# Gated DeltaNet core: masked decay matrices made and stored in the projection

## What is computed

```python
decay = where(tril, exp(g[:, None] - g[None, :]), 0)
L  = where(strict, (k * beta) @ k.T * decay, 0)     # solve (I + L) [u, w] = [v*beta, k*beta*exp(g)]
qk = where(tril, q @ k.T * decay, 0)
q_dec = q * exp(g)
v_new = u - w @ S
o  = q_dec @ S + qk @ v_new
S  = S * exp(g_last) + k_dec.T @ v_new
```

## Time and profile before

| | |
|---|---|
| median of 3 runs | 4827.85 us (4827.19 to 4833.41) |
| the profiled execution, its own time | 4825.45 us |
| its span | 4823.7 us |
| busy, share of the span | PE 86%, PEld 71%, DVE 57%, ACT 43%, POOL 37% |
| mean granted TensorE clock | 0.954 |
| HBM read, written | 369.87 MB, 169.54 MB |
| GDN projection | about 247 to 1562 us |
| delta core | about 1585 to 3310 us |

### The profile page before, as it was taken

How to read it: one execution, slowest core, us unless ns; L and a number is a source line. 1 busy time by engine, 2 the same in 40 slices (tenths; PEclk the granted TensorE clock), 3 DMA queues, 4 the chain that set the end, 5 groups by cost and what they waited for, 6 DMA issues and landing times. The chain is left out here.

```text
span 4823.7 us, 83518 instructions
## 1 busy us (share of the span) xinstructions
PE 4166.8 (86%) x30756; PEld 3447.5 (71%) x30756; DVE 2754.4 (57%) x3377; ACT 2085.9 (43%) x3927; POOL 1768.6 (37%) x1236
## 2 busy tenths in 40 slices
PE   7699999999999688888888888884999779978769
PEld 2278888888887577777777777774888668866657
DVE  3245454554545677777777777775455433228853
ACT  3222222223232566666666666664111421128832
POOL 2222121221211567666777677664111232200022
PEclk8799999999999799999999999997999789998889
DMA  6212221222222444444444444434444324253244
GB/s 224 87 44 76 78 74 57 68 79 74 64 67 68 117 112 112 113 112 114 115 114 111 114 113 111 111 108 159 169 175 176 116 75 142 97 217 137 113 138 136
DMA packets 598327, 541.17 MB, mean 112 GB/s; under 512 B 118688, under 2 KB 562336, under 8 KB 581024
## 3 DMA queue, kind: packets, MB, share of 16 engines
q1 hardware_dynamic: 598208, 539.59, 36.3%
HBM read 369.87 MB, written 169.54 MB: 112 GB/s over the span
## 5 line engine op out<-in xcount | busy, mean ns | idle before, releaser
L555 PE MATMUL pj_bank<-h_hi,pj_whi 128*128 128x512 f32 (+1 forms) x1920 | 717.1, 373 | 19.9 <-POOL pj_wlo L541 18.8
L555 PE MATMUL pj_bank<-h_lo,pj_whi 128*128 128x512 f32 (+1 forms) x1920 | 708.3, 369 | 0.0
L555 PE MATMUL pj_bank<-h_hi,pj_wlo 128*128 128x512 f32 (+1 forms) x1920 | 707.5, 368 | 0.0
L745 ACT ACTIVATE pj_raw<-pj_bank 128x512 f32<-128x512 f32 (+1 forms) x240 | 127.9, 553 | 952.5 <-PE pj_bank L555 473.5
L538 POOL TENSOR_TENSOR pj_whi<-pj_w,ones 128x1024 fp32r<-128x1024 f32 x48 | 115.3, 2402 | 1021.4 <-PE pj_bank L555 1007.1
L555 PEld LDWEIGHTS pj_bank<-h_hi,pj_whi 128*128 128x128 f32 x1920 | 363.3, 189 | 84.3 <-POOL pj_wlo L541 19.3
L1368 DVE TENSOR_TENSOR dc_Y<-dc_psY,dc_pick 128x256 f16<-128x256 f32 x864 | 323.1, 415 | 168.0 <-PE dc_psY L1119 168.0
L1274 ACT ACTIVATE dc_R<-dc_psR 128x256 f16<-128x256 f32 x720 | 245.3, 382 | 396.7 <-PE dc_psR L1135 395.6
L555 PEld LDWEIGHTS pj_bank<-h_lo,pj_whi 128*128 128x128 f32 x1920 | 363.4, 189 | 62.3 <-issue 3.8
L555 PEld LDWEIGHTS pj_bank<-h_hi,pj_wlo 128*128 128x128 f32 x1920 | 363.0, 189 | 60.7
L838 DVE TENSOR_SCALAR pj_acc<-pj_raw,pj_conv_w 128x2307 f32<-128x2307 f32 x32 | 90.8, 2836 | 471.1 <-ACT pj_raw L745 471.1
(11 more groups left out here) (270 smaller groups left out, 10396.6 us busy)
## 6 DMA issues: line engine op xcount, KB each, us to landing
dc_tm<-scratch_tm SPq DMA_DIRECT2D x288, 192.0 KB, 2.5
dc_cgr<-scratch_cgrow SPq DMA_DIRECT2D x288, 128.0 KB, 2.8
dc_fm<-scratch_fm SPq DMA_DIRECT2D x288, 128.0 KB, 2.3
scratch_o<-dc_ob SPq DMA_DIRECT2D x288, 128.0 KB, 2.0
scratch_tm<-pj_tm SPq DMA_DIRECT2D x24, 1152.0 KB, 5.0
pj_w<-in_gdn_w_in SPq DMA_DIRECT2D x48, 512.0 KB, 6.2
scratch_fm<-pj_row SPq DMA_DIRECT2D x16, 1152.0 KB, 5.2
dc_kr<-scratch_fm SPq DMA_DIRECT2D x288, 64.0 KB, 2.6
```

What stands on the lines that cost most here:

```text
L555: i = pe.matmul(self.bank[blk][:, 0:n], l[b][:, k, :], r[:, k, at:at + n], start=(m == 0), stop=(m == 3 * KT - 1))
L745: act.activation(raw_row(raw, blk), pr.bank[blk][:, 0:BLKS[blk][1]], ACT.Silu if KINDS[j] == "z" else ACT.Copy).then_inc(pr.s_ev, 1)
```

## The change

- **Gates:** ScalarE also makes Exp of the rows `cgT` (five groups), which SyncE stores as `egrow` in two pieces before the last store of the phase.
- **Projection:** every tile also makes the decays of three chunks (8 heads x 18 chunks = 144 items in all): SyncE loads the broadcast rows and the gates of the chunk; ScalarE makes Abs of the difference (four of 128 columns, the gate as bias) and Exp; VectorE multiplies by beta and the strict mask (four of 128 columns) into `BD` and by the inclusive mask into `E`; SyncE stores both to DRAM (`decays`). On ScalarE decays 0 and 1 stand ahead of a tile's first `take`, decay 2 ahead of its last; on VectorE all three stand ahead of the tile's convolution or normalisation.
- **`Projection`** (both projections): the raw weights share memory with the low part, so the load waits for TensorE's products of the tile two back; the high part is a plain copy.
- **Core:** differences, Abs, Exp, beta and mask multiplies are gone. SyncE loads `dd` (both decay matrices) and `egr` (the exponentiated row). VectorE makes L and QK straight from the Gram bank, one behind the other, at levels 1 and 2; TensorE reuses the bank after QK. QK has four buffers. ScalarE's high parts move from levels 4 and 5 to 2 and 3; GpSimd keeps `Sd`, `qd`, `vb` and `Llo`. A and the first X stay on VectorE as they were.

```diff
@@ Projection
-        if not first:
-            sp.wait_ge(self.s_split, t - 1)
+        if not first:
+            sp.wait_ge(self.s_mm, t * NB - NB)
...
-        pool.tensor_tensor(self.whi[b][:], self.w32[b][:], self.ones[:].unsqueeze(1).broadcast_to([P, KT, P]),
-                           ALU.mult).then_inc(self.s_whi, 1)
+        pool.tensor_copy(self.whi[b][:], self.w32[b][:]).then_inc(self.s_whi, 1)
@@ phase_project_gdn, SyncE
+                def decays(h, j, last):
+                    store_decay(h, j, 0)
+                    store_decay(h, j, 1)
+                    load_decay(h, j, 2)
...
+                    if not done:
+                        load_decay(*then, 0)
+                    store_decay(h, j, 2)
+                    if not done:
+                        load_decay(*then, 1)
@@ phase_project_gdn, ScalarE
+                def decay(h, j, o):
+                    c, b, k, u = item(h, j, o)
+                    act.wait_ge(d_load[b], u * 48 + 48)
+                    for dr in range(2):
+                        for v in range(2):
+                            i = act.activation(E[b][:, dr, v], E[b][:, dr, v], ACT.Abs, scale=-1.0, bias=gi[b][:, dr, Q_CG, v:v + 1])
+                    i.then_inc(s["d_abs"], 1)
+                    act.wait_ge(s["d_abs"], k + 1)
+                    act.activation(E[b][:], E[b][:], ACT.Exp, scale=-1.0).then_inc(s["d_exp"], 1)
...
                 def stage(h, j, first):
+                    decay(h, j, 0)
+                    decay(h, j, 1)
                     take(h, j, 0, first)
...
+                    decay(h, j, 2)
                     take(h, j, 4, first)
@@ phase_project_gdn, VectorE
+                def decay(h, j, o):
+                    c, b, k, u = item(h, j, o)
+                    dve.wait_ge(s["d_exp"], k + 1)
+                    for dr in range(2):
+                        for v in range(2):
+                            i = dve.scalar_tensor_tensor(BD[b][:, dr, v], E[b][:, dr, v], gi[b][:, dr, Q_BETA, v:v + 1], strict[:, dr],
+                                                         ALU.mult, ALU.mult)
+                    i.then_inc(s["d_scaled"], 1)
+                    dve.wait_ge(s["d_scaled"], k + 1)
+                    dve.tensor_tensor(E[b][:], E[b][:], incl[:].unsqueeze(2).broadcast_to(C4), ALU.mult).then_inc(s["d_done"], 1)
...
                 def stage(h, j, first):
+                    for o in range(PT):
+                        decay(h, j, o)
@@ phase_delta_core, GpSimd
+                    if rec:
+                        for p in range(2):
+                            faded_state(i, q, p)
+                    if inv:
+                        for p in range(2):
+                            faded_q(i + 1, 1 - q, p)
                     for p in range(2):
+                        if inv:
+                            beta_v(i + 1, 1 - q, p)
                         if make:
                             low(i + 2, q, p)
@@ phase_delta_core, TensorE
                     else:
-                        pe.wait_ge(s_gm[0], j + 1)
+                        pe.wait_ge(s_qk[0], j + 1)
...
                     if p == 0:
-                        wait(pe, s_gm[1], i + 3, NI)
+                        wait(pe, s_qk[1], i + 3, NI)
@@ phase_delta_core, VectorE
-                def masked(j, q, p):
...
-                    dve.tensor_tensor(gm[q][p][:], bV[:], sides[:], ALU.mult).then_inc(s_gm[p], 1)
-
-                def scores(j, q, p):
-                    dve.wait_ge(s_bd[p], j + 1)
+                def scores(j, q, r, p):
+                    dve.wait_ge(p_gram[p], j + 1)
+                    dve.wait_ge(ld_d[q][p], of_load(j, q, 2))
                     wait(dve, s_llo[p], j)
-                    dve.wait_ge(s_gm[p], j + 1)
-                    dve.tensor_tensor(L32[p][:], heads(gm[q][p][:, :, 0, :]), bd[p][:], ALU.mult).then_inc(s_L[p], 1)
+                    dve.tensor_tensor(L32[p][:], heads(bV[:, :, 0, :]), dd[q][p][:, :, 1], ALU.mult).then_inc(s_L[p], 1)
+                    wait(dve, p_out[p], j - 3)
+                    dve.tensor_tensor(qk[r][p][:], heads(bV[:, :, 1, :]), dd[q][p][:, :, 0], ALU.mult).then_inc(s_qk[p], 1)
...
                         if make and l in (1, 2):
-                            masked(i + 2, q, l - 1)
+                            scores(i + 2, q, (r + 2) % 4, l - 1)
                         if rec and l == 2:
                             right_side(i, q, 1)
-                        if make and l in (3, 4):
-                            scores(i + 2, q, l - 3)
```

More of the change, by code:

```diff
@@ L353, in _ @@
                 sp.dma_start(dram["cgrow"], cgT[:]).then_inc(s["stored"], 16)
+                sp.wait_ge(s["grown"], len(GROUPS))
+                for at in range(0, TOK, HALF):
+                    n = min(HALF, TOK - at)
+                    sp.dma_start(dram["egrow"][:, at:at + n], grown(at, n)).then_inc(s["stored"], 16)
                 sp.wait_ge(s["pack"], 1)
@@ L442, in _ @@
                 i.then_inc(s["el"], 1)
+                act.wait_ge(s["rows"], KT)
+                for n, at, w in GROUPS:
+                    act.wait_ge(s["row"], n + 1)
+                    act.activation(grown(at, w), cgT[:, at:at + w], ACT.Exp).then_inc(s["grown"], 1)
             @block.vector
@@ L592, in phase_project_gdn @@
         epsq = sb("epsq", [P, 1])
+        C4 = [P, 2, 2, P]
+        E, BD = ([sb(f"{x}{i}", C4) for i in range(2)] for x in ("E", "BD"))
+        gi = [sb(f"gi{i}", [P, 2, NQTY, 2]) for i in range(2)]
+        incl, strict = sb("incl", [P, 2, P], F16), sb("strict", [P, 2, P], F16)
+        dram["decays"] = nc.dram_tensor("scratch_decays", (NQ, NCH, 2, P, 2, 2, P), F32, kind="Internal").ap()
+        d_load, d_out = ([sem(f"pj_d_{x}{i}") for i in range(2)] for x in ("load", "out"))
         aux = [ctx.enter_context(nc.psum_tensor(f"pj_aux{i}", [P, 512], F32)) for i in range(3)]
         names = ("const", "conv0", "conv1", "conv2", "conv", "pads", "silu", "square", "aux", "aux_read", "recip", "norm",
-                 "fm_out", "tm_out", "z_out", "fm_turn")
+                 "fm_out", "tm_out", "z_out", "fm_turn", "sides", "mask", "d_abs", "d_exp", "d_scaled", "d_done")
         s = {q: sem("pj_" + q) for q in names}
@@ L662, in stage @@
                         store_tm(h, "trK", 0)
+                    decays(h, j, last)
                 for j in range(NT):
@@ L674, in _ @@
                 sp.wait_ge(s["z_out"], 32 * nth(NQ - 1, NT - 1, "z"))
+                for b in range(2):
+                    sp.wait_ge(d_out[b], 32 * (NQ * NCH // 2))
             @block.gpsimd
@@ L884, in phase_delta_core @@
         Rf = two("Rf", C4)
-        qk, qd = four("qk", C4), four("qd", C4)
+        qk, qd = [[sb(f"qk{r}{p}", C4) for p in range(2)] for r in range(4)], four("qd", C4)
         vb, xr, vs, vn, ob, Sd = (two(x, C4) for x in ("vb", "xr", "vs", "vn", "ob", "Sd"))
@@ L1000, in step @@
                 def step(m, n, last):
-                    for load, ahead in ((load_rec, 1), (load_fm, 3), (load_row, 4)):
+                    for load, ahead in ((load_rec, 1), (load_fm, 3), (load_decays, 4)):
                         if not (last and n + ahead >= NCH):
@@ L1210, in run @@
                 @sweep
-                def run(i, q, ahead, make, inv, rec):
-                    j, r = i + 1, 1 - q
+                def run(i, q, r, make, inv, rec):
+                    j = i + 1
                     for l in range(1, NLEV):
@@ L1296, in run @@
                 @sweep
-                def run(i, q, ahead, make, inv, rec):
+                def run(i, q, r, make, inv, rec):
                     j = i + 1
-                    if make:
-                        decays(i + 2, q, 0)
                     for l in range(1, NLEV):
@@ L1309, in run @@
                             new_v(i, l - 3)
-                        if make:
-                            if l == 1:
-                                decays(i + 2, q, 1)
-                            elif l <= 3:
-                                growth(i + 2, q, l - 2)
-                            elif l <= 5:
-                                high(i + 2, l - 4)
+                        if make and l in (2, 3):
+                            high(i + 2, l - 2)
                     if rec:
```

164 lines of the change are left out of this document (78 added, 86 removed).

## The result

The changed kernel takes **5023.48 us** (median of 4 runs, 5018.29 to 5025.51) against 4830.44 for the kernel before in the same comparison (4827.19 to 4833.41): a ratio of **1.0398**, 95% interval 1.038 to 1.0416. The forecast was 4891, its range 4802 to 4955. The sign was right; the size was three times what I had.

The account below looks back on a forecast made before the run. The projection was taken as bound by TensorE's products, the delta core by hand-overs with no engine full. Core 25, opening -3, projection 40 and gates 1 gave +63 us on the median 4827.85: 4891 us, range 4802 to 4955.

Parts of the forecast that it names:

- Core, the walk: Delta core step: hand-over delay of 1.2 us less 0.84 us from a shorter X, so 0.36 us a step longer.
- The term of the X: Core, VectorE: first X no longer beside GpSimd's subtraction, 0.42 us instead of 1.26, state 0.84 us earlier.
- The dearer hand-over: Core: two VectorE multiplies instead of one after each Gram product before bank reuse, 1.2 us later at level 3.
- rival 2: Core: freed VectorE swallows the second multiply and the whole 0.88 us wait goes; total 4804 us, chance 0.18.
- rival 3: Core: VectorE not freed of GpSimd, X stays 1.26 us; core +84, total 4950 us, chance 0.14.
- over some 70 steps: Delta core: the 0.36 us of one step multiplied over the core's steps, +25 us.
- I take 5 us a head, eight heads: +40 us: Projection: third decay delays the convolution of K by 4 to 6 us, stalling TensorE; bounds 0 and 72.
- the walk's own terms: Projection, one head: normalisation ends 979.1, decays 0 and 1 by 982.9, decay 2's load lands 988 to 990 us.
- behind it stand silu and square: Projection, after K's late convolution: both end at 1005.82, TensorE's norms begin at 1005.9, so no slack.
- a tile that I had called free: Projection: in tiles Q and V decay 2 was to end about 0.7 us before the convolution.
- None before the norms of Q: Projection: no TensorE idle time expected before the norms of Q, against about 5 us a head before K's.
- The table loads: Projection, ScalarE: 1.28 us each by the row used; at the skill's 2.66, eight heads cost an estimated 11 us more.

Follow-up runs that it names:

- experiment 7: Changed kernel with three row-load buffers, one Gram-bank copy at the hand-over (GpSimd makes QK, loop of two) and second L cast at level 3: 4744.76 us.
- experiment 1: Kernel before with four steps instead of two in the delta core's loop body on every engine: 4870.55 us (1.0083).
- experiment 8: Kernel before, core loop body lengthened: four steps on TensorE only 4872.22 us; four on the other engines only 4831.01; eight on all 4846.31.
- experiment 9: Changed kernel with TensorE's core program written out for all 72 steps, other engines keeping the loop of four: 4963.88 us (1.0277).
- Experiment 4: Changed kernel with three buffers for the projection's loaded rows and two half-size beta buffers: 4884.36 us (1.0112).

## Why the prediction was wrong, and where it was right

**Core, the walk: right.** "1.2 - 0.84 = 0.36 us a step". The term of the X is shown by itself: 0.84 from the one cast. The dearer hand-over has no run of its own; against the kernel of experiment 7 it is 1.20 (23.75 against 22.55), with the other differences named there. The net of the two was 0.19 a step (23.75 against 23.56), 14 us instead of 25. The kernel before is 1.01 above that of experiment 7 and not 0.84, so 0.17 us a step are left that no run assigns. Rivals 2 and 3 are refused by the rows: the second multiply was not swallowed, and VectorE was freed.

**Core, the loop: missed.** The prediction priced "over some 70 steps" by one step and never looked at what the body of four does to TensorE's own program. It costs 50 us of the 62.5, and experiments 1, 8 and 9 show it from both sides. The profile of before could have warned: the 71 step lengths of its core (1625 to 3299 us) hold 17738 matmul and 17735 weight-load records, 500 a step.
**Projection: right in kind, mis-sized by three.** "I take 5 us a head, eight heads: +40 us". Against the start of the tile behind it (TensorE's first product of Z1: 986.46 in the head of the walk, 1054.65 in the one shown above), the walk's own terms held up to the load: normalisation over 7.2 us ahead of that tile (I had 7.4), both decays done 3.6 ahead (3.6). The load did not: I had it landed 1.5 to 3.5 us after the tile's start, it landed 5.1 after; two row loads took 1.99 us to issue and not 0.86. The convolution began 8.85 after the tile's start where it had begun 0.95 after, so it was 7.9 late and not 4 to 6; it then ran 9.7 us and not 13.2, which I had not counted either, and ended 4.4 late. So this chain is worth 4.4 us in the head shown, near the 5 of the forecast, but by two errors against each other.

The step of the projection that failed is the next one: "behind it stand silu and square". What stands between is the decay of the next tile's chunk 1, with a chain of its own (landing at 1072.60), and I never walked it. It adds 2.6 us in tile Z1 and makes most of the stall in a tile that I had called free: in the tile Z0 before it the convolution of Q ended at 1010.51, 14.4 us after the tile's start where it had been 14.1, but the decay of chunk 1 landed at 1010.59, and the evacuation came at 1013.85, 3.3 behind; TensorE stood 3.6 us before the norms of Q. Mean tile lengths, before and after: Z0 29.5 and 33.1, Z1 29.5 and 37.4, V1 27.0 and 32.7, with K and V0 unchanged: 17 us a head (V1 without the last one of the phase). "None before the norms of Q" is refused. And each stall was paid twice, since TensorE's clock fell behind it (0.50 from 1081 to 1085 us, behind the 7.09): 38 of the 136 us are the same products, run slower.

**The table loads.** The row and the Trainium skill (ScalarE: Activation LUTs, "What ACT_TABLE_LOAD costs") differed, 1.28 and about 2.66 us. In the changed kernel Exp, table load and evacuation follow one another (1073.92, 1074.57, 1075.86): the load starts as the Exp ends, and the next operation 1.29 us later. No further drain is to be seen, and the trace speaks for the row. Experiment 4 has all the table loads and loses nothing.

## What to carry to other kernels

Count the buffers against the chunks of a tile, and walk the buffer's round (store, receipt, load, landing) for every use in the order in which the in-order engines meet it, the first of the next tile too: two buffers for three chunks cost 136 us here, one more for the loaded rows cost no time and gave it all back, with ScalarE just as busy. Before unrolling a loop count TensorE's instructions in its body. And what an edit frees (here VectorE, of GpSimd) can be kept while its price is sent back: the same precomputed decays with one copy at the hand-over, three loads and the short loop make 4744.76 us, 1.8% under the kernel before.

## What the hardware showed that I had not expected

- TensorE waits for its own instructions at the head of a long body, on the jump back: 1.7 to 2.4 us. Elsewhere in a core, and in every core with a body of two steps or none, no such wait was over 0.7 us.
- The rest of a long step is the granted clock, and it does not fall behind every such wait. Of the 15 long steps of the changed kernel ten have a stretch of 3.4 us at 0.50 (1.2 GHz) and are 3.4 to 4.1 us longer; five stay at 1.00 and are 2.0 to 2.3 longer, the one at 1955 us with a wait of 1.95 where the one shown had 1.80. The same stretch comes without a wait as well: two steps of the kernel before have it (from 1766.7 and 3087.9 us) and are 1.6 and 1.9 us longer. What decides it no run shows.
- VectorE beside GpSimd goes by who came first. With GpSimd's cast of the weights begun at 1074.33 and its subtraction behind it, four small multiplies begun at 1074.93 took 4.08 us instead of 1.13:

```profile
1074.33 1.58 POOL L549 CAST pj_whi<-pj_wlo_raw 128x1024 fp32r<-128x1024 f32 x1 [29.37 <-DMA pj_wlo_raw<-in_gdn_w_in]
1075.98 2.35 POOL L551 TENSOR_TENSOR pj_wlo<-pj_wlo_raw,pj_whi 128x1024 fp32r<-128x1024 f32 x1
```

```profile
1074.93 4.08 DVE L908 SCALAR_TENSOR_TENSOR pj_BD<-pj_E,pj_gi,pj_strict 128x128 f32<-128x128 f32 x4
```

  The cast itself, 1.04 us elsewhere, took 1.58 beside a VectorE multiply begun 0.01 us before it. In return the convolution's three two-input passes went from a mean of 3237 to 2622 ns and its first pass from 2877 to 1415 (before: 300 to 1560 us, after: 300 to 1600), as GpSimd's splits now come at another time: of the 32 first passes of before, 30 overlapped one and took 2.8 to 3.4 us, the two others 1.42, as all 32 do now. The Trainium skill (SBUF — State Buffer, "Who interferes with whom") says that the two share a pair of ports, that a VectorE instruction with two inputs in SBUF contends with one of GpSimd that reads there, and that the order of issue decides who is held; the rows agree.
